# A fused attention layer's first phase: the latents are turned by VectorE in 32x32 blocks and moved in shares, no longer transposed by TensorE

## The reference

```python
xn = rms_norm(h, norm_in[l])
proj = jnp.einsum('bsd,dn->bsn', xn, w_in[l])          # 2464 columns
a_q, a_k, a_v, a_g, b_cq, b_ckv, b_kr, b_g = jnp.split(proj, _SPLITS, axis=-1)
...
c_q = rms_norm(b_cq, b_cq_norm[l])                     # the query latent, 384 wide
c_kv = rms_norm(b_ckv, b_ckv_norm[l])                  # the key/value latent, 256 wide
qb = jnp.einsum('bsr,rn->bsn', c_q, w_uq[l])           # 4 heads of 96
kvb = jnp.einsum('bsr,rn->bsn', c_kv, w_ukv[l])        # 4 heads of 64 + 128
...                                                    # head norms, rotations
y_a = blocked_attention(q, k, v)                       # 8 grouped heads of 64
y_b = blocked_attention(qb, kb, vb)                    # 4 latent heads
y = jnp.concatenate([y_a * jax.nn.silu(a_g), y_b * jax.nn.silu(b_g)], axis=-1)
h = h + jnp.einsum('bsm,md->bsd', y, w_out[l])
```

## Time and profile before

| | |
|---|---|
| median of three runs | 1584.38 us (1583.38 to 1584.66) |
| the profiled execution | 1581.66 us, its span 1579.9 us |
| PE busy | 1534.4 us, 97% |
| DVE busy | 1303.0 us, 82% |
| ACT busy | 1232.3 us, 78% |
| POOL busy | 586.0 us, 37% |
| phase 1, to the last matmul's start | 491.14 us |
| phase 2's first matmul | 493.66 us |

### The profile page before, as it was taken

The page is one execution under the profiler, slowest core; times in us unless marked ns, Lnnn a source line. Parts: engine busy times, 40 slices in busy tenths (PEclk is TensorE's granted clock), DMA queues, the critical chain, the costliest instruction groups (busy, mean ns, idle before and its releaser), DMA issues.

```text
span 1579.9 us, 37686 instructions
## 1 busy us (share of the span) xinstructions
PE 1534.4 (97%) x13326; PEld 889.6 (56%) x13326; DVE 1303.0 (82%) x1947; ACT 1232.3 (78%) x1656; POOL 586.0 (37%) x506
## 2 busy tenths in 40 slices
PE   7999999999998999999999999999999999979999
PEld 3555555555553566566566556656655655644444
DVE  6886676776888988998898899899889889897764
ACT  8787667667657888888888888888888888877663
POOL 0100000000002665666666566666656656630000
PEclk9999999999999999999999999999999999999999
DMA  9344444453323543334323334323332422536663
GB/s 339 109 137 76 112 116 71 109 110 70 82 65 98 112 99 72 86 82 96 79 64 92 79 79 97 86 65 70 83 66 63 92 58 67 125 91 213 201 198 106
DMA packets 245540, 162.51 MB, mean 103 GB/s; under 512 B 65040, under 2 KB 226320, under 8 KB 245488
## 3 DMA queue, kind: packets, MB, share of 16 engines
q1 hardware_dynamic: 222128, 147.28, 37.2%
q10 hardware_dynamic: 22464, 13.63, 3.1%
q0 software_dynamic: 896, 0.93, 0.8%
HBM read 119.16 MB, written 40.93 MB: 101 GB/s over the span
## 4 chain that ended last, share of the span: by engine, by line
PE 56%; DVE 8%; issue 3%; ACT 0%; DVEq 0%; DMA 0%; POOLq 0%; SPq 0%
PE p_acc L2063 5%; PE p_st L2027 5%; PE p_st L2026 5%; PE p_acc L2067 4%; DVE hand_part L1864 4%; PE hand_mx L1994 4%; PE p_acc L2069 4%; PE p_acc L2068 3%; PE p_st L1507 3%; PE p_st L1508 3%; PE p_st L1510 3%; PE p_st L2029 3%; PE p_st L2030 3%; PE hand_mx L1996 3%; PE p_acc L2064 3%
## 5 line engine op out<-in xcount | busy, mean ns | idle before, releaser
L1776 POOL TENSOR_TENSOR p_pl<-p_p,p_ph 128x512 f16<-128x512 f32 x384 | 503.9, 1319 | 291.6 <-ACT p_ph L1815 232.3
L1864 DVE TENSOR_REDUCE hand_part<-hand_mx 128x2 f32<-128x1024 f32 x373 | 455.0, 1220 | 78.1 <-PE hand_mx L1994 60.0
L1806 ACT ACTIVATE p_p<-p_st 128x1024 f32<-128x1024 f32 x384 | 390.9, 1018 | 98.3 <-PE p_st L2034 50.2
L1194 PE MATMUL p_ring<-p_w_hi,p_xT 128*128 128x512 f16 (+3 forms) x1536 | 389.3, 339 | 7.5 <-DVE p_w_lo L902 5.0
L1815 ACT ACTIVATE p_ph<-p_p 128x1024 f16<-128x1024 f32 x336 | 355.2, 1057 | 18.4
L1892 DVE TENSOR_TENSOR p_pl<-p_p,p_ph 128x512 f16<-128x512 f32 x384 | 325.9, 849 | 5.4 <-ACT p_ph L1815 4.6
L1194 PE MATMUL p_ring<-p_w_lo,p_xT 128*128 128x512 f16 (+3 forms) x768 | 260.0, 339 | 0.0
L1194 PEld LDWEIGHTS p_ring<-p_w_hi,p_xT 128*128 128x128 f16 x1536 | 150.7, 98 | 127.1 <-DVE p_xT L860 5.6
L2063 PE MATMUL p_acc<-p_vas,p_ph 128*128 128x129 f16 x2048 | 207.9, 221 | 0.0
L2063 PEld LDWEIGHTS p_acc<-p_vas,p_ph 128*128 128x128 f16 x2048 | 180.6, 97 | 36.4 <-issue 14.1
L2064 PE MATMUL p_acc<-p_vas,p_pl 128*128 128x65 f16 x2048 | 201.1, 193 | 0.0
(11 more groups left out here) (196 smaller groups left out, 2364.8 us busy)
## 6 DMA issues: line engine op xcount, KB each, us to landing
p_vbs<-scratch_vb SPq DMA_DIRECT2D x16, 1028.0 KB, 6.3
p_xin<-in_x SPq DMA_DIRECT2D x16, 512.0 KB, 7.1
p_xcol<-in_x_cols SPq DMA_DIRECT2D x16, 512.0 KB, 6.7
scratch_g<-p_g SPq DMA_DIRECT2D x16, 512.0 KB, 3.4
p_kb<-scratch_kb SPq DMA_DIRECT2D x32, 256.0 KB, 5.4
p_vas<-in_x SPq DMA_DIRECT2D x16, 512.0 KB, 4.0
out<-p_ph SPq DMA_DIRECT2D x15, 512.0 KB, 2.8
out_gt<-scratch_g ACTq DMA_DIRECT2D x13, 512.0 KB, 3.4
```

The source lines that it names most:

```text
L1194: last = pe.matmul(ring_t[:, 0:w], a, b, start=(k == 0 and m == 0), stop=(k == len(steps) - 1 and m == len(terms) - 1))
L1776: pool.tensor_tensor(pl[:, s % NP, 1, :], p32[:, s % N32, QB:], ph[:, s % NP, 1, :], ALU.subtract).then_inc(s_lop, 1)
L1806: act.activation(p32[:, s % N32, :], st[:, s % 2, :, :].rearrange("p a b -> p (a b)"), ACT.Exp, scale=scale).then_inc(s_exp, 1)
L1864: dve.tensor_reduce(part[:, e // MPAIRS % 3, 2 * c:2 * c + 2], mx[:, :, :], AX, ALU.max).then_inc(s_red, 1)
```

## The change

TensorE no longer turns the latents. The new order of a tile's latents is:

- `latent_scale` (ScalarE): the scaled latents stay float32, in place, in `cq32` and `ckv32`.
- `latent_turn` (VectorE): two block transposes, 128x384 and 128x256, into a part of the rotation's work tile `T2`.
- `latent_hi` (ScalarE) rounds the turned 128x640 to the first half of `lat`, and `latent_lo` (VectorE) makes the second by a subtraction.
- `latent_move`: 16 instructions of 32x320 move the blocks of both halves to `latT`; ScalarE has quadrants 2 and 3 (eight), VectorE 0 and 1 (eight). `up` waits for both.

Of the heads' blocks ScalarE now moves quadrant 3 alone, and does so after `gate(t, "bg")` at the end of its tile; VectorE moves 0, 1 and 2. In T14 VectorE moves the latents ahead of `z_lo`; in T15 it makes `latent_lo` ahead of `rotate_heads`, and ScalarE moves the latents ahead of `z_hi`.

```diff
+        def latent_moves(quadrants):
+            halves = lat[:, :, :].rearrange("p s (k q t) -> p (s k) q t", k=5, q=4)
+            for g, d in moves(quadrants):
+                yield latT[32 * d:32 * d + 32, :, 32 * g:32 * g + 32], halves[32 * g:32 * g + 32, :, d, :]
...
 # ScalarE
-            def z_move(t, h, pr, c0=0, c1=NCH, quadrants=(2, 3)):
+            def z_move(t, h, pr, c0=0, c1=NCH, quadrants=(3,)):
-            def latents_turned(t):
-                act.wait_ge(s_lph, t + 1)
-                act.activation(latT[:, 0:5, :], turned_hi[:, 0:5, :], ACT.Copy).then_inc(s_lth, 1)
+            def latent_move(t):
+                act.wait_ge(s_dlat, t * 3 + 3)
+                if not zero(t):
+                    act.wait_ge(s_proj, turn(t - 1, "ukv1") + 1)
+                for dst, src in latent_moves((2, 3)):
+                    last = act.activation(dst, src, ACT.Copy)
+                last.then_inc(s_lta, 1)
-            def latent_hi(t, h):
+            def latent_scale(t, h):
+                act.wait_ge(s_dlat, t * 3 + 1)
+                act.activation(cq32[:, h, :], cq32[:, h, :], ACT.Copy, scale=ls[:, 4:5])
+                act.activation(ckv32[:, h, 0:RKV], ckv32[:, h, 0:RKV], ACT.Copy, scale=ls[:, 5:6]).then_inc(s_lat, 1)
+            def latent_hi(t):
+                act.wait_ge(s_dlat, t * 3 + 2)
...
+                act.activation(lat[:, 0, :], turned_lat, ACT.Copy).then_inc(s_lat, 1)
...
 # ScalarE, tile
-                latent_hi(t, h)
+                latent_scale(t, h)
                 if not last:
+                    latent_hi(t)
                     z_hi(t - 1, 1 - h)
                     x_hi(t + 1, 1 - h)
                     aq_out(t, h)
                     akv_out(t, h)
-                    latents_turned(t)
-                    z_move(t - 1, 1 - h, i if h == 1 else i - 1)
+                    latent_move(t)
                     gate(t, "ag")
...
                 if not last_tiles(t):
                     gate(t, "bg")
+                if not last:
+                    z_move(t - 1, 1 - h, i if h == 1 else i - 1)
...
 # VectorE
-            def z_move(t, h, pr, c0=0, c1=NCH, quadrants=(0, 1)):
+            def z_move(t, h, pr, c0=0, c1=NCH, quadrants=(0, 1, 2)):
+            def latent_turn(t, h):
+                dve.wait_ge(s_lat, t * 6 + 5)
+                dve.transpose(turned_lat[:, 0:RQ], cq32[:, h, :])
+                dve.transpose(turned_lat[:, RQ:], ckv32[:, h, 0:RKV]).then_inc(s_dlat, 1)
+            def latent_lo(t):
+                dve.wait_ge(s_lat, t * 6 + 6)
...
+                dve.tensor_tensor(lat[:, 1, :], turned_lat, lat[:, 0, :], ALU.subtract).then_inc(s_dlat, 1)
...
 # VectorE, tile
                 x_rstd(t + 2, h)
+                latent_turn(t, h)
                 x_scale(t + 1, 1 - h)
-                latent_lo(t, h)
+                latent_lo(t)
                 z_lo(t - 1, 1 - h)
                 x_lo(t + 1, 1 - h)
-                latents_turned(t)
+                latent_move(t)
                 z_move(t - 1, 1 - h, i if h == 1 else i - 1)
...
 # VectorE, last_pair
                 if h == 0:
+                    latent_turn(T14, 0)
                     x_scale(T15, 1)
-                    latent_lo(T14, 0)
+                    latent_lo(T14)
+                    dve.wait_ge(s_dlat, T14 * 3 + 3)
                     rotate_heads(T13, 1)
+                    latent_move(T14)
                     z_lo(T13, 1)
-                    latents_turned(T14)
                     x_lo(T15, 1)
...
                 else:
+                    latent_turn(T15, 1)
+                    latent_lo(T15)
+                    dve.wait_ge(s_dlat, T15 * 3 + 3)
                     rotate_heads(T14, 0)
-                    latent_lo(T15, 1)
...
-                    latents_turned(T15)
+                    latent_move(T15)
                     z_lo(T14, 0)
...
 # TensorE
-            def turn_latents(t):
...
             def up(t, new):
-                pe.wait_ge(s_lth, t + 1)
-                pe.wait_ge(s_ltl, t + 1)
+                pe.wait_ge(s_lta, t + 1)
+                pe.wait_ge(s_ltd, t + 1)
```

More of the change, by code:

```diff
@@ L313, in phase1 @@
         s_ident = sem("identity_ready")
[L314 to L317, removed]
+        s_lta = sem("latent_quadrants_moved_act")
+        s_ltd = sem("latent_quadrants_moved_dve")
         s_R = sem("R_written")
@@ L770, in first_pair @@
                 split_hi(6, 0)
+                latent_hi(1)
                 up_out(0, 0)
@@ L805, in tile @@
                     akv_out(t, h)
-                    latents_turned(t)
-                    z_move(t - 1, 1 - h, i if h == 1 else i - 1)
+                    latent_move(t)
                     gate(t, "ag")
                 elif h == 0:
+                    latent_hi(T14)
                     aq_out(T14, 0)
@@ L812, in tile @@
                     z_hi(T13, 1)
-                    latents_turned(T14)
-                    z_move(T13, 1, PAIRS - 2, quadrants=(3,))
+                    latent_move(T14)
+                    z_move(T13, 1, PAIRS - 2)
                     x_hi(T15, 1)
@@ L817, in tile @@
                 else:
+                    latent_hi(T15)
                     akv_out(T15, 1)
@@ L878, in z_move, with latent_move @@
                 last.then_inc(s_ztd, 1)
-            def latents_turned(t):
-                dve.wait_ge(s_lpl, t + 1)
-                dve.tensor_copy(latT[:, 5:10, :], turned_lo[:, 0:5, :]).then_inc(s_ltl, 1)
+            def latent_move(t):
+                dve.wait_ge(s_dlat, t * 3 + 3)
+                if not zero(t):
+                    dve.wait_ge(s_proj, turn(t - 1, "ukv1") + 1)
+                for dst, src in latent_moves((0, 1)):
+                    last = dve.tensor_copy(dst, src)
+                last.then_inc(s_ltd, 1)
             def k14_lo():
@@ L1098, in first_pair @@
                 split_lo(4, 0)
-                latent_lo(0, 0)
+                latent_turn(0, 0)
                 split_lo(4, 1)
+                latent_lo(0)
                 latent_rstd(1, 1)
-                split_all(5)
-                latents_turned(0)
-                latent_lo(1, 1)
+                split_lo(5, 0)
+                latent_move(0)
+                split_lo(5, 1)
+                latent_turn(1, 1)
                 x_rstd(2, 0)
                 split_all(6)
+                latent_lo(1)
                 split_lo(7, 0)
@@ L1109, in first_pair @@
                 v_lo(0)
-                latents_turned(1)
+                latent_move(1)
                 split_lo(7, 1)
@@ L1304, in last_pair @@
                     proj_in(T14, 0, "akv", False)
-                    turn_latents(T14)
                     proj_in(T13, 1, "bg", False)
@@ L1309, in last_pair @@
                     proj_in(T15, 1, "aq", False)
-                    turn_latents(T15)
                     proj_in(T14, 0, "ag", False)
```

73 lines of the change are left out of this document (24 added, 49 removed).

## The result

The changed kernel takes 1623.7 us (median, 1621.4 to 1627.2), the kernel before 1584.4 in the same comparison: ratio 1.0251, 95% interval [1.0239, 1.0264]. The forecast was 1597.4, with 1592 to 1604 as range. The direction was right and 26 us were missing. The profiled execution of after took 1627.2 us (span 1625.4), 3.5 more than the median; all of the loss is there when phase 2 begins (540.27 us, against 493.66 before).

What follows compares the result with a forecast made beforehand. TensorE was taken to bound tiles 4 to T13, other engines the ends of phase 1. Terms +8.4 - 1.4 - 5.5 + 3.3 + 5.8 = +10.6, plus 2.4 of clock, on 1584.4 gave 1597.4 us, range 1592 to 1604.

Steps and rivals of the forecast that it cites:

- `up` of tile 2: First pair and tile 2: `up` of tile 2 starts at 105.8 in place of 97.39, a loss of 8.4 us.
- tile 3's step, its clock included: Tile 3 follows tile 2 after 28.4 us, not 29.8 (-1.4); half clock behind tile 2 costs 1.7.
- tiles 4 to 13: In the loop, TensorE saves 0.55 us of transposes in each of ten tiles: a gain of 5.5 us.
- T14: At T14, ScalarE's latent moves end at 446.75, where `up` started at 443.41: a loss of 3.3 us.
- T15: At T15, the serial chain makes `up` 9.1 us later, 3.3 of it T14's: a loss of 5.8 us.
- behind `up` of T15, its clock: After T15's long TensorE wait, half clock costs 0.7 us, as half of its loss falls on another wait.
- ScalarE full in the first pair: In the first pair ScalarE's additions add up, less two waits: +4.9 us at the roots that release VectorE.
- Slack of 0.7 us on ScalarE in the loop: In tiles 4 to 13, ScalarE keeps 0.7 us of slack before TensorE wants the latents, so the 0.55 is gained.
- Clock: Long idle stretches of TensorE before tile 2's `up` and in T15 each bring half clock: +2.4 us, bounds 0 and 5.
- clock stays up: Rival: TensorE's clock does not fall behind the long waits, so only +10.6 us, 1595.0 us; chance 0.18.
- The loop loses its slack: Rival: VectorE's moves cost 0.47 us each, making latents late in every loop tile: about +19, 1603.5 us; chance 0.12.
- Faster: Rival: first pair and tail absorb their additions, leaving TensorE's 16 times 0.55, -8.8: 1575.6 us; chance 0.05.

Runs made afterwards that it cites:

- number 1: The changed kernel with ScalarE's move of the heads (quadrant 3) put back in front of the evacuation of `ag`: 1597.4 us, ratio 1.0086.
- number 3: The kernel before, latents turned on TensorE, with ScalarE moving heads' quadrant 3 at the tile's end and VectorE quadrants 0 to 2: 1602.9 us.
- number 4: The kernel before with only the share changed: VectorE moves heads' quadrants 0 to 2, ScalarE quadrant 3, at the old place: 1584.5 us.
- number 11: The kernel before, with only tiles 2 and 3 written out in front of the loop, as a control: 1585.4 us, ratio 1.0001.
- number 6: The changed kernel with the early heads' move, but TensorE turns the first pair's latents as before: 1593.4 us, ratio 1.0058.
- number 8: The changed kernel, early heads' move, block turn in tiles 2 to 13 only, both ends as before, old share of heads' moves: 1628.9 us.
- number 2: The changed kernel, but SP issues an even tile's v and gate stores ahead of the pair's fourteen stores: 1598.7 us, ratio 1.0094.
- number 10: The changed kernel, but in odd tiles SP waits for the gate's store before issuing the next loads: 1611.5 us, ratio 1.0175.
- number 5: The changed kernel with the early heads' move, block turn in tiles 2 to 13 only, both ends as before, new share: 1585.4 us.
- 7: The changed kernel with the early heads' move, but TensorE turns T14's and T15's latents in the old order: 1588.7 us, ratio 1.003.
- 9: The changed kernel with the early heads' move, block turn and new share in tiles 4 to 13 only, other tiles as before: 1576.7 us.

## Why the prediction was wrong

The step that failed is this one: "`z_move` at ScalarE's tile end (four at 466, 1.9 us) takes idle time; the stores of the pair, now issued about 10 us later, are next waited for by VectorE's moves a tile on, where more than 10 us are left. Cost 0; at worst one wait of 1 us." Its first half holds: the four moves take 1.90 us and the pair's stores are later, by 8.1 us against `up` (11.3 for 3.2 in number 1). I then asked only who waits for these stores, and not what is queued behind them on SP. The gate's store is, and `gate(t, "ag")` waits for it. The term measured 26.3 us (number 1 against after) in place of 0, and 18.4 without the block turn (number 3 against number 4). None of my rivals had this mechanism, and the range had no room for it.

In the profile of after it divides so: tiles 4, 6, 8, 10 and 12 are together 28.6 us later than in number 1 by their steps; 18.0 of that are TensorE's five waits, and the other 10.6 fit the half clock behind each (1.5 to 3.0; 1.56 in tile 8, more where half clock lasts longer). T13's wait adds 1.3. The rest of the 32.0 us between the two at `up` of T15 lies in the first pair and tile 3, most of it (1.6) at `up` of tile 0 already.

The other terms, by number 1, which has all of the change but the late place (1597.4 us measured, 1597.4 forecast):

| term | forecast | number 1 |
|---|---|---|
| `up` of tile 2 | +8.4 | +8.2 (105.58) |
| tile 3's step, its clock included | -1.4 + 1.7 | +0.9 (30.70) |
| tiles 4 to 13 | -5.5 | -5.6 |
| T14 | +3.3 | +3.4 |
| T15 | +5.8 | +5.9 |
| behind `up` of T15, its clock | +0.7 | +2.8 |
| phase 2's first matmul | +13.0 | +15.6 (509.27) |

That the time agrees to the tenth is luck in part. By the profile the sum missed by 2.6 us: the clock behind tile 2 cost 2.3 (30.70 against 28.41), not 1.7, and that of T15 2.8, not 0.7. It is at half for some 5.6 us behind `up` of T15; the forecast reckoned with 3.4 in all, half of it hidden. Number 1's rows:

```profile
484.00:488.00 4.00, 4.00 (x14) 1.88 (x13) 3.88 (x13) 0.49 (x1) 0.00 (x0) 0.50 0.10 24
```
```profile
509.27 0.41 PE L2006 MATMUL hand_mx<-early 64*128 64x512 f16 x2 [2.15 <-PEq L234]
```

This miss doesn't show in the time, since the sum was taken from one profiled execution of before and added to a median 2.7 us above it. In that execution the clock stayed up in T15. In the profile of number 11, whose work is the same, it fell there and ahead of tile 2's `up`, and phase 2 began at 495.98 instead of 493.66.

The inside of tile 2's term is also off in places that cancel. `up` of tile 0 was 0.5 us earlier in number 1 (41.67 for 42.20), so by its own count the term is 8.7. The roots' release of VectorE was at 67.56 there, +4.5 for +4.9. VectorE's share is the 1.5 that I took (number 4).

- *ScalarE full in the first pair*: right. Its two waits of the earlier trace rows are gone, and number 6 gives back 4.1 us.
- *The end*: the path is right, its clock is not. TensorE waits 3.84 us in T14 and 5.9 (number 1) or 6.28 (after) in T15, where 6.3 was forecast. But "from there to phase 2 all is as before" is wrong: that stretch is 23.0 us in every kernel with the old order there and 24.8 to 25.9 in every one with the new.
- *Slack of 0.7 us on ScalarE in the loop*: right, and tighter than I made of it. In number 1 the latents' moves of tile 7 end at 249.27 and `up` starts at 249.93; the moves of heads behind them stand before `ag`, and number 8 shows what 3.6 us more there do.
- *Clock*: right that long idle stretches bring it down, too small in number, since the forecast had two such stretches and after has one more in each pair, and since it priced that of T15 at a quarter of what it cost.
- *Rivals*: "clock stays up" fell (0.50 behind tile 2). "The loop loses its slack" by dearer VectorE moves fell (232 ns). "Faster" fell with the two ends.

## What to carry to other kernels

When an instruction that lets go a transfer is moved, list the whole queue behind that transfer and who waits for each entry; the transfer's own reader may be the one with the most time. A change that wins in the steady loop and loses where the pipeline fills and drains is worth splitting: tiles 4 to 13 alone won 7 us where all tiles, with the move early, lost 13. When landing times of one line are compared, take apart the transfers that someone waits for: the median over all tiles hid that the waited ones took 11.8 us and the others 2.6. Price an engine's slack at each evacuation that the bound engine needs, not once a tile: one quadrant of moves before `ag` made the difference between 1585 and 1629 us.

## What the runs showed of the hardware

- Landing time depends on when a store is issued. The even tiles' gate store of 512 KB took 4.3 us at the median before, 4.5 in number 1 and 3.2 in number 2. It took 11.8 in after, 10.8 in number 3, and 10.3 in number 10, where no load went beside it. In after and in number 10 it was in flight while the DMA engines moved 31 to 78 GB/s.
- Waits of TensorE of the same length bring half clock or don't. It followed all five waits of after in the loop (2.61 to 4.43 us). In number 8 it followed waits of 2.96 us, at 201.40 and 266.13, and not the one of 2.91 at 234.58, which is why its steps alternate (33.2 and 31.5); yet it followed 2.53 at 429.73. The wait of 2.3 us in T15 is in eight of the profiles: the clock fell behind it in numbers 5, 7, 8 and 11 (steps of 28.9 to 29.2 us) and did not in before and in numbers 3, 4 and 9 (27.2). Rows of 460 to 470 us, before and then number 5:

```profile
460.00:470.00 10.00, 7.66 (x44) 3.71 (x43) 8.72 (x23) 3.67 (x9) 0.00 (x0) 1.00 0.44 142
```
```profile
460.00:470.00 10.00, 7.67 (x36) 3.40 (x35) 8.72 (x24) 3.35 (x7) 0.00 (x0) 0.83 0.47 146
```

  What decides between the two stays open. It may be why number 5 spreads from 1580.6 to 1586.6 us; no run tells. Two profiles of the same work can differ by some 2 us for it, so a sum of that size can't be read from one of them.
